# A third weight slab joins the block-by-block start of the two feed-forward layers of an RWKV-7 and pooling decoder step

## The chip, the core and the metric

The kernel runs on one core of a Trainium2 chip, as one program. The metric is the device time in microseconds; lower is better. It is written in Bass: every engine has its own instruction stream, written by hand, and the streams meet only at semaphores that count upwards. TensorE is called PE below, VectorE DVE, ScalarE ACT, GpSimd POOL, and SP is the queue that issues the weight loads.

## What is computed

One inference step of a two-layer trunk for a prompt of 256 tokens and 8 sequences of 4 new tokens, so T = 288 columns. Layer 0 mixes with RWKV-7, layer 1 with causal pooling, and a SwiGLU feed-forward network follows each of them. After every sublayer the residual sum is normalised. Cut to what matters here:

```python
D_MODEL, D_FF = 2048, 5632

def _layer_norm(x, g, b):
    mu = jnp.mean(x, axis=-1, keepdims=True)
    var = jnp.mean(jnp.square(x - mu), axis=-1, keepdims=True)
    return (x - mu) * lax.rsqrt(var + LN_EPS) * g + b

def _swiglu(x, w_in, w_down):
    h = x @ w_in
    gate, up = h[..., :D_FF], h[..., D_FF:]
    return (jax.nn.silu(gate) * up) @ w_down

# in each layer i, after the mixer has given h:
x = _layer_norm(ALPHA * x + h, ln_g[i, 0], ln_b[i, 0])            # norm 0 or norm 2
x = _layer_norm(ALPHA * x + _swiglu(x, ffn_w_in[i], ffn_w_down[i]), ...)
```

## The kernel before

**Layout.** Activations stand with the model dimension on the partitions: X is 16 blocks of 128 x 288. Every matrix product is made from two halves of each operand: the high half is the value rounded to the fp32r type, the low half is the rest. So one 128x128 block of weights times one 128x288 block of activations is three matmuls, written by the helper `three` (lines 727, 728, 729): high x high, high x low, low x high.

**Slabs.** `ffn_w_in` is read in slabs of 2048 x 128 (1 MB): a slab holds the weights of one block of 128 hidden columns, gate and up parts by turns. SP loads slab s into RAW[s % 4] as soon as the low half of slab s - 4 has been taken. ACT writes the high half into WH[:, s % 2] (`hi`, line 1253), and DVE the low half into WL[:, s % 2] (`lo`, line 1683). Since WH and WL have two places, `hi` of slab s waits until PE has used slab s - 2: `act.wait_ge(slab_used, s + 1)`. PE increments `slab_used` with the last matmul of a slab. PE waits for the low half of slab s in `take_slab`. A slab is 16 blocks times 3 matmuls, 48 matmuls.

**The start of a feed-forward layer.** The first three slabs are called s0, s0 + 1 and s0 + 2. Slabs s0 and s0 + 1 stand in the two places of WH and WL. Slab s0 + 2 has places of its own, W3H and W3L, which exist at this one point of each layer. ACT writes W3H in the middle of the norm (`third_hi`, line 1520). DVE writes W3L in `third_lo` (line 2237), after everything that it does for the norm. Slab s0 + 3 goes into WH[:, 1] and WL[:, 1], the place of slab s0 + 1.

**The norms 0 and 2** (`layer_norm`) stand between the mixer and the feed-forward layer. DVE subtracts the mean, ACT squares, PE sums the squares over the partitions (line 1100), ACT takes the root (line 1534), DVE the reciprocal (line 2088). While the root is made, DVE converts what `beside` names: two slabs at norm 0, one slab at norm 2. Then the norm is applied block by block, 16 times: DVE scales (line 2093), ACT adds the bias and writes the high half MH (lines 1538 and 1540), DVE writes the low half ML (line 2098) and increments `ln_lo`. PE follows behind: for each block k it waits for `ln_lo` and then makes the three matmuls of block k for slab s0 and the three for slab s0 + 1. After all 16 blocks it makes slab s0 + 2 in one piece (`third_slab`), and then slab s0 + 3 (`hidden(0, 3)`), which is the first that went through the ordinary rotation of two places.

**Behind it.** ACT takes the sigmoid of each gate block (line 1558), DVE multiplies twice (lines 2180, 2183), ACT and DVE write the halves HH and HL of the hidden block (lines 1560, 2188). ACT's order at the start is: `hi` of s0 + 3, sigmoid, HH, `hi` of s0 + 4, `hi` of s0 + 5.

Of the kernel before, what the change touches and what calls it, by code (L numbers as in the profile page):

```python
# [25 lines left out]
T = SEQ + NS  # L26
# [106 lines left out]
def build(nc, x_prompt, x_sample, state_wkv, state_shift, state_pool, ln_g, ln_b, rw_mu, rw_wr, rw_wk, rw_wv,  # L133
# [4 lines left out]
    with ctx:  # L138
# [585 lines left out]
        def _(pe):  # L724
            def three(out, wh, wl, xh, xl, first, last):

                pe.matmul(out, wh, xh, start=first, stop=False)  # L727
                pe.matmul(out, wh, xl, start=False, stop=False)  # L728
                return pe.matmul(out, wl, xh, start=False, stop=last)  # L729

            def take_slab(s):
                pe.wait_ge(lo_ready, s + 5)

            def take_bank(o):
                pe.wait_ge(out_free, o + 1)
# [388 lines left out]
            def ffn(layer, lnk):  # L1124
                for g in range(2):
                    s0 = SLAB[f"ffn{layer}"] + g * FFN_SLABS
                    o0 = OUT[f"ffn{layer}"] + g * FFN_OUTS

                    def up(j, k):
                        return three(PS[j][:, 0:T], WH[:, j % 2, k * P:(k + 1) * P], WL[:, j % 2, k * P:(k + 1) * P],  # L1130
                                     MH[0][:, k, :], ML[0][:, k, :], k == 0, k == KC - 1)

                    def hidden(i, j):
                        take_slab(s0 + 4 * i + j)
                        take_bank(o0 + 4 * i + j)
                        for k in range(KC):
                            ins = up(j, k)
                        ins.then_inc(slab_used, 1)

                    def third_slab():  # L1140
                        take_slab(s0 + 2)
                        take_bank(o0 + 2)
                        for k in range(KC):
                            ins = three(PS[2][:, 0:T], W3H[:, k * P:(k + 1) * P], W3L[:, k * P:(k + 1) * P],
                                        MH[0][:, k, :], ML[0][:, k, :], k == 0, k == KC - 1)
                        ins.then_inc(slab_used, 1)

                    if g == 0:

                        take_slab(s0 + 1)  # L1150
                        take_bank(o0 + 1)
                        for k in range(KC):
                            pe.wait_ge(ln["lo"], HALVED[lnk] + k + 1)
                            first = up(0, k)
                            second = up(1, k)
                        first.then_inc(slab_used, 1)
                        second.then_inc(slab_used, 1)
                        third_slab()
                        hidden(0, 3)
                    with pe.Fori(1 - g, HG // 2) as i:  # L1160
                        for j in range(4):
                            hidden(i, j)
                    s1, o1 = s0 + 2 * HG, o0 + 2 * HG
                    hidden_before = 2 + (2 * layer + g) * HG
                    pe.wait_ge(hl_ready, hidden_before + HH2)

                    def outputs(i, js):
                        for j in js:
                            c = 4 * i + j // 2
                            take_slab(s1 + 8 * i + j)  # L1170
                            if j % 2 == 0:
                                take_bank(o1 + c)
                            for k in range(HH2):
                                kk = (j % 2) * HH2 + k
                                if kk == HG - 1 and isinstance(i, int):
                                    pe.wait_ge(hl_ready, hidden_before + HG)
                                ins = three(PS[j // 2][:, 0:T], WH[:, j % 2, k * P:(k + 1) * P],
                                            WL[:, j % 2, k * P:(k + 1) * P], HH[:, kk, :], HL[:, kk, :],
                                            kk == 0, kk == HG - 1)
                            ins.then_inc(slab_used, 1)  # L1180
                            if g == 1 and isinstance(i, int) and i > 0 and j == 0:
                                pe.wait_ge(st["x"], 15 * layer + 12)
                                pe.matmul(PS[4][:, 0:T], AVG, SUM[:, :], start=True, stop=True).then_inc(st["c"], 1)

                    outputs(0, range(8))
                    with pe.Fori(1, KC // 4 - g) as i:
                        outputs(i, range(8))
                    if g == 1:
                        outputs(KC // 4 - 1, range(8))
# [489 lines left out]
        def _(dve):  # L1679
# [397 lines left out]
            def layer_norm(k, beside):  # L2077
                n = k // 2
                dve.wait_ge(ln["mean"], n + 1)
                for q in range(4):  # L2080
                    xs = X[:, 4 * q:4 * q + 4, 1:T + 1]
                    dve.tensor_tensor(xs, xs, PS[4][:, 0:T].unsqueeze(1).broadcast_to([P, 4, T]), ALU.subtract)\
                       .then_inc(ln["cen"], 1)
                dve.wait_ge(ln["sq"], 4 * n + 4)
                dve.tensor_tensor(SQ[:, 8:12, :], SQ[:, 8:12, :], SQ[:, 12:16, :], ALU.add).then_inc(ln["pairs"], 1)
                beside()
                dve.wait_ge(ln["sd"], 2 * n + 2)
                dve.reciprocal(LNS[:, 1, :], LNS[:, 0, :]).then_inc(ln["rstd"], 1)
                dve.wait_ge(ln["rstd"], n + 1)
                dve.wait_ge(ln["cen"], 4 * n + 4)  # L2090

                def scaled(c):
                    dve.scalar_tensor_tensor(out=xcur(c), in0=xcur(c), scalar=par("ln_g", k * KC + c),
                                             in1=LNS[:, 1, :], op0=ALU.mult, op1=ALU.mult).then_inc(ln["scaled"], 1)

                def low(c):
                    dve.wait_ge(ln["done"], n * KC + c + 1)
                    dve.tensor_tensor(one(ML[0], c), xcur(c), one(MH[0], c).bitcast(F32), ALU.subtract)\  # L2098
                       .then_inc(ln["lo"], 1)

                for c in range(3):
                    scaled(c)
                with dve.Fori(0, KC - 3) as c:
                    scaled(c + 3)
                    low(c)
                for c in range(KC - 3, KC):
                    low(c)
                third_lo(SLAB["ffn0"] if k == 0 else SLAB["ffn1"])

            def four(q):  # L2110
                return X[:, 4 * q:4 * q + 4, 1:T + 1]
# [123 lines left out]
            def third_lo(s0):  # L2235
                dve.wait_ge(hi_ready, s0 + 3)
                dve.tensor_tensor(W3L[:, :], RAW[:, 2, :], W3H[:, :].bitcast(F32), ALU.subtract).then_inc(lo_ready, 1)
# [127 lines left out]
```

## Time and profile before

| what | value |
|---|---|
| median of 3 runs | 2696.5 us (2691.27 to 2697.71) |
| the profiled execution's own time | 2698.18 us |
| its span in the profile | 2696.6 us |
| PE busy | 2580.0 us, 96% of the span |
| DVE busy | 1577.9 us, 59% |
| ACT busy | 1131.9 us, 42% |
| mean granted PE clock | 0.981 of full |
| chain that ended last | PE 82%, DVE 11%, ACT 3% |

How to read it: PE is the engine that sets the time. A microsecond counts when PE stands still or runs at a lower clock; time on DVE or ACT counts only where PE waits for it. The profile's own time is 1.7 us above the median, within the scatter of the runs. All times below are microseconds from the span's start. Norm 0 lies at about 885 to 917, norm 2 at about 1814 to 1845.

### The profile page before, as it was taken

How to read it: one execution, taken by the hardware profiler on the slowest of the kernel's cores; microseconds unless marked ns; L12 is line 12 of the kernel's file. 1: busy time of each engine (PE TensorE's matmuls, PEld its weight loads, DVE VectorE, ACT ScalarE, POOL GpSimd, SP SyncE). 2: the span in 40 equal slices, each digit the busy share in tenths (PEclk: the TensorE clock that was granted, in tenths of full speed). 3: DMA queues.
4: the chain of work that ended last, by engine and by line, in shares of the span. 5: the costliest groups of instructions: out<-in, count | busy, mean ns of one | idle time of the engine just before them, and what ended most of it. 6: DMA issues, size and time to landing. Idle time of an engine off the chain costs nothing.

```text
span 2696.6 us, 56357 instructions
## 1 busy us (share of the span) xinstructions
PE 2580.0 (96%) x23305; PEld 2480.2 (92%) x23305; DVE 1577.9 (59%) x2400; ACT 1131.9 (42%) x1596; POOL 142.5 (5%) x211
## 2 busy tenths in 40 slices
PE   7989999999999899999999999969999999999997
PEld 7977888888789899999999999958999999999997
DVE  7877888888856644444444444686444444444446
ACT  5565555555533533333333333445333333333334
POOL 0000111111001000000000000100000000000000
PEclk9989999999999999999999999979999999999999
DMA  7622223222336656555665556524555566565563
GB/s 211 184 78 71 77 83 84 84 84 82 91 91 196 156 164 169 161 146 162 188 171 161 166 141 168 175 69 125 165 161 166 144 167 190 160 170 163 142 167 94
DMA packets 707051, 379.33 MB, mean 141 GB/s; under 512 B 16023, under 2 KB 699191, under 8 KB 706711
## 3 DMA queue, kind: packets, MB, share of 16 engines
q1 hardware_dynamic: 701040, 363.46, 48.1%
q0 software_dynamic: 5792, 13.34, 1.8%
q8 instruction: 114, 1.87, 0.3%
q10 hardware_dynamic: 70, 0.39, 0.1%
q14 instruction: 35, 0.29, 0.0%
HBM read 367.31 MB, written 10.62 MB: 140 GB/s over the span
## 4 chain that ended last, share of the span: by engine, by line
PE 82%; DVE 11%; ACT 3%; issue 2%; DMA 1%; SPq 0%; DVEq 0%; POOL 0%; ACTq 0%
PE PS L727 25%; PE PS L728 24%; PE PS L729 24%; PE PS L880 2%; DVE WL L1683 2%; ACT WH L1253 1%; DVE PL L1800 1%; DVE ML L1698 1%; PE PS L912 1%; DVE TM L1691 1%; DMA PR<-in_rw_wk 1%; PE PS L999 0%; PE PS L954 0%; PE PS L917 0%; DVE XL L1939 0%
## 5 line engine op out<-in xcount | busy, mean ns | idle before, releaser
L1683 DVE TENSOR_TENSOR WL<-RAW,WH 128x2048 fp32r<-128x2048 f32 (+1 forms) x325 | 658.6, 2027 | 761.0 <-ACT WH L1253 761.0
L727 PE MATMUL PS<-MH,WH 128*128 128x288 f32 (+1 forms) x3152 | 931.2, 295 | 17.8 <-DVE ML L2098 11.8
L728 PE MATMUL PS<-ML,WH 128*128 128x288 f32 (+1 forms) x3152 | 933.7, 296 | 0.0
L729 PE MATMUL PS<-MH,WL 128*128 128x288 f32 (+1 forms) x3152 | 932.9, 296 | 0.0
L1253 ACT ACTIVATE WH<-RAW 128x2048 fp32r<-128x2048 f32 (+1 forms) x325 | 553.4, 1703 | 824.7 <-PE PS L729 808.5
L727 PEld LDWEIGHTS PS<-MH,WH 128*128 128x128 f32 (+1 forms) x3152 | 595.8, 189 | 22.3 <-issue 13.8
L728 PEld LDWEIGHTS PS<-ML,WH 128*128 128x128 f32 (+1 forms) x3152 | 595.8, 189 | 0.2
L729 PEld LDWEIGHTS PS<-MH,WL 128*128 128x128 f32 (+1 forms) x3152 | 595.0, 189 | 0.0
L728 PE MATMUL PS<-HL,WH 128*128 128x288 f32 x1408 | 415.3, 295 | 0.0
L729 PE MATMUL PS<-HH,WL 128*128 128x288 f32 x1408 | 415.0, 295 | 0.0
L727 PE MATMUL PS<-HH,WH 128*128 128x288 f32 x1408 | 413.4, 294 | 0.0
L727 PEld LDWEIGHTS PS<-HH,WH 128*128 128x128 f32 x1408 | 264.7, 188 | 0.1
L728 PEld LDWEIGHTS PS<-HL,WH 128*128 128x128 f32 x1408 | 264.7, 188 | 0.1
L729 PEld LDWEIGHTS PS<-HH,WL 128*128 128x128 f32 x1408 | 264.5, 188 | 0.0
L727 PE MATMUL PS<-MH,PH 128*128 128x288 f32 x768 | 245.5, 320 | 8.4 <-DVE ML L2028 3.8
L728 PE MATMUL PS<-ML,PH 128*128 128x288 f32 x768 | 230.0, 300 | 0.0
L729 PE MATMUL PS<-MH,PL 128*128 128x288 f32 x768 | 229.1, 298 | 0.0
L727 PEld LDWEIGHTS PS<-MH,PH 128*128 128x128 f32 x768 | 147.2, 192 | 33.5 <-issue 22.2
L728 PEld LDWEIGHTS PS<-ML,PH 128*128 128x128 f32 x768 | 147.7, 192 | 0.3
L1560 ACT ACTIVATE HH<-TM 128x288 f32 (+1 forms) x88 | 39.2, 445 | 258.6 <-DVE TM L2183 258.6
L729 PEld LDWEIGHTS PS<-MH,PL 128*128 128x128 f32 x768 | 147.5, 192 | 0.0
L1800 DVE TENSOR_TENSOR PL<-PR,PH 128x512 fp32r<-128x512 f32 x144 | 92.5, 653 | 51.3 <-ACT PH L1354 50.3
(313 smaller groups left out, 2726.7 us busy)
## 6 DMA issues: line engine op xcount, KB each, us to landing
RAW<-in_ffn_w_in SPq DMA_DIRECT2D x176, 1024.0 KB, 5.7
RAW<-in_ffn_w_down SPq DMA_DIRECT2D x128, 704.0 KB, 4.8
RAW<-in_rw_wr SPq DMA_DIRECT2D x16, 1024.0 KB, 6.5
PR<-in_rw_wk SPq DMA_DIRECT2D x64, 256.0 KB, 3.1
PR<-in_rw_wv SPq DMA_DIRECT2D x64, 256.0 KB, 3.0
PR<-in_rw_wo SPq DMA_DIRECT2D x64, 256.0 KB, 3.2
S0N<-in_state_wkv POOLq DMA_DIRECT2D x64, 64.0 KB, 2.2
out<-SOS POOLq DMA_DIRECT2D x64, 64.0 KB, 2.7
```

The costliest lines, as they stand in the source:

```text
L727: pe.matmul(out, wh, xh, start=first, stop=False)
L728: pe.matmul(out, wh, xl, start=False, stop=False)
L729: return pe.matmul(out, wl, xh, start=False, stop=last)
L880: ins = pe.matmul(bank[hr[r], col + u * CH:col + (u + 1) * CH], lhs(hr[r], u), rhs(hr[r], u), start=True, stop=True)
L912: pe.transpose((PA, PB)[t][:, n * P:(n + 1) * P], f[:, t * P:(t + 1) * P], IDN)
L1253: act.activation(WH[0:rows, j % 2, 0:n], RAW[0:rows, j, 0:n], ACT.Copy).then_inc(hi_ready, 1)
L1560: act.activation(HH[:, bass.ds(hc, 1), :].rearrange("p a t -> p (a t)"), TM[:, b, :], ACT.Copy).then_inc(hh_ready, 1)
L1683: dve.tensor_tensor(WL[0:rows, j % 2, 0:n], RAW[0:rows, j, 0:n], WH[0:rows, j % 2, 0:n].bitcast(F32), ALU.subtract).then_inc(lo_ready, 1)
L1691: dve.scalar_tensor_tensor(out=TM[:, c % 2, :], in0=XX[:, c, :], scalar=PAR[:, row:row + 1], in1=X[:, c, 1:T + 1], op0=ALU.mult, op1=ALU.a ...
L1698: dve.tensor_tensor(ML[m][:, c, :], mixed, MH[m][:, c, :].bitcast(F32), ALU.subtract)\
L1800: dve.tensor_tensor(PL[slot][0:rows, 0:n], PR[slot][0:rows, 0:n], PH[slot][0:rows, 0:n].bitcast(F32), ALU.subtract).then_inc(pc_lo, 1)
```

## The change

Two edits, both at the start of the two feed-forward layers. On PE, slab s0 + 2 no longer follows in one piece: each block now makes nine matmuls, three for each of the slabs s0, s0 + 1, s0 + 2. The matmuls that increment `slab_used` for the three slabs are therefore the last ones of block 15 for each slab. The waits for W3L (`take_slab(s0 + 2)`) and for the third PSUM bank stand ahead of the first block. On DVE, `third_lo` moves from the end of `layer_norm` to the place between `beside()` and the reciprocal. ACT's and SP's streams are the same as before.

```diff
                     if g == 0:
 
-                        take_slab(s0 + 1)
-                        take_bank(o0 + 1)
+                        take_slab(s0 + 2)
+                        take_bank(o0 + 2)
                         for k in range(KC):
                             pe.wait_ge(ln["lo"], HALVED[lnk] + k + 1)
-                            first = up(0, k)
-                            second = up(1, k)
-                        first.then_inc(slab_used, 1)
-                        second.then_inc(slab_used, 1)
-                        third_slab()
+                            ends = [up(0, k), up(1, k), third(k)]
+                        for ins in ends:
+                            ins.then_inc(slab_used, 1)
                         hidden(0, 3)
...
                 beside()
+                third_lo(SLAB["ffn0"] if k == 0 else SLAB["ffn1"])
                 dve.wait_ge(ln["sd"], 2 * n + 2)
                 dve.reciprocal(LNS[:, 1, :], LNS[:, 0, :]).then_inc(ln["rstd"], 1)
...
                 for c in range(KC - 3, KC):
                     low(c)
-                third_lo(SLAB["ffn0"] if k == 0 else SLAB["ffn1"])
```

DVE's stream at norm 0, before the change (LNS is the norm's scale, ML the low half of the normalised block):

```order
L1683 TENSOR_TENSOR WL<-RAW,WH 128x2048 x2
L2088 RECIPROCAL LNS<-LNS 128x288
L2093 SCALAR_TENSOR_TENSOR X<-X,PAR,LNS 128x288 x3
...
L2098 TENSOR_TENSOR ML_61<-X,MH_60 128x288 x3
L2237 TENSOR_TENSOR W3L<-RAW,W3H 128x2048
L1683 TENSOR_TENSOR WL<-RAW,WH 128x2048
L2180 TENSOR_TENSOR TM<-TM,PS 128x288
```

DVE's stream at the same place, after the change (its line numbers are five lower):

```order
L1678 TENSOR_TENSOR WL<-RAW,WH 128x2048 x2
L2232 TENSOR_TENSOR W3L<-RAW,W3H 128x2048
L2084 RECIPROCAL LNS<-LNS 128x288
L2089 SCALAR_TENSOR_TENSOR X<-X,PAR,LNS 128x288 x3
...
L2094 TENSOR_TENSOR ML_61<-X,MH_60 128x288 x3
L1678 TENSOR_TENSOR WL<-RAW,WH 128x2048
L2175 TENSOR_TENSOR TM<-TM,PS 128x288
```

The low half W3L moved from behind the last ML to the place ahead of the reciprocal. Norm 2 has the same two streams with one WL in place of two at the top.

PE's stream at the end of the 16 blocks of norm 0, before (PS0 to PS3 are the banks of the slabs s0 to s0 + 3):

```order
L727 MATMUL PS1<-MH0_60,WH_50 128x288
L728 MATMUL PS1<-ML0_61,WH_50 128x288
L729 MATMUL PS1<-MH0_60,WL_51 128x288
L727 MATMUL PS2<-MH0_60,W3H_175 128x288
L728 MATMUL PS2<-ML0_61,W3H_175 128x288
...
L729 MATMUL PS2<-MH0_60,W3L_176 128x288
L727 MATMUL PS3<-MH0_60,WH_50 128x288
L728 MATMUL PS3<-ML0_61,WH_50 128x288
```

The same place after the change:

```order
L728 MATMUL PS1<-ML0_61,WH_50 128x288
L729 MATMUL PS1<-MH0_60,WL_51 128x288
L727 MATMUL PS2<-MH0_60,W3H_175 128x288
L728 MATMUL PS2<-ML0_61,W3H_175 128x288
L729 MATMUL PS2<-MH0_60,W3L_176 128x288
L727 MATMUL PS3<-MH0_60,WH_50 128x288
L728 MATMUL PS3<-ML0_61,WH_50 128x288
```

Between the last matmul of slab s0 + 1 (PS1) and the first of slab s0 + 3 (PS3) there stood 48 matmuls of slab s0 + 2; now there stand 3.

## Rows read from the trace of the kernel before

**Rows 1.** Costliest groups: busy, mean ns of one | idle before, releaser

```profile
L1683 DVE TENSOR_TENSOR WL<-RAW,WH 128x2048 fp32r<-128x2048 f32 (+1 forms) x325 | 658.6, 2027 | 761.0 <-ACT WH L1253 761.0
L1253 ACT ACTIVATE WH<-RAW 128x2048 fp32r<-128x2048 f32 (+1 forms) x325 | 553.4, 1703 | 824.7 <-PE PS L729 808.5
```

**Rows 2.** PE's waits over the whole span: us in total, times, longest

```profile
PE PS L727 <- DVE ML L2098: 11.8, 2, 6.2
```

**Rows 3.** Timeline, head of norm 0: start, us, engine, line [idle before <-releaser]

```profile
893.51 4.49 DVE L1683 TENSOR_TENSOR WL<-RAW,WH 128x2048 fp32r<-128x2048 f32 x2
...
896.81 0.44 ACT L1534 ACTIVATE LNS<-LNS 128x288 f32<-128x288 f32 x1
897.92 1.95 DVE L2088 RECIPROCAL LNS<-LNS 128x288 f32<-128x288 f32 x1
...
902.53 0.58 PE L727 MATMUL PS<-MH,WH 128*128 128x288 f32 x1 [6.20 <-DVE ML L2098]
```

**Rows 4.** Timeline, head of norm 2

```profile
1822.12 2.28 DVE L1683 TENSOR_TENSOR WL<-RAW,WH 128x2048 fp32r<-128x2048 f32 x1
...
1825.90 1.95 DVE L2088 RECIPROCAL LNS<-LNS 128x288 f32<-128x288 f32 x1 [1.49 <-ACT LNS L1534]
...
1830.50 0.58 PE L727 MATMUL PS<-MH,WH 128*128 128x288 f32 x1 [5.56 <-DVE ML L2098]
```

**Rows 5.** Timeline, the blocks of norm 0 and their end

```profile
909.02 0.45 DVE L2098 TENSOR_TENSOR ML<-X,MH  x1
...
909.89 0.45 DVE L2098 TENSOR_TENSOR ML<-X,MH  x1
...
914.86 2.28 DVE L2237 TENSOR_TENSOR W3L<-RAW,W3H 128x2048 fp32r<-128x2048 f32 x1
...
916.97 0.29 PE L729 MATMUL PS<-MH,WL 128*128 128x288 f32 x1
...
917.20 0.40 PE L727 MATMUL PS<-MH,W3H 128*128 128x288 f32 x1
...
917.37 1.92 ACT L1253 ACTIVATE WH<-RAW 128x2048 fp32r<-128x2048 f32 x1 [2.91 <-PE PS L729]
```

**Rows 6.** Timeline, where slab s0 + 2 begins at norm 2

```profile
1845.28 0.30 PE L727 MATMUL PS<-MH,W3H 128*128 128x288 f32 x1
```

**Rows 7.** Windows: stretch, length, busy of PE, PEld, DVE, ACT, POOL, PEclk, DMA

```profile
907.00:917.00 10.00, 10.00 (x78) 10.00 (x76) 9.28 (x18) 7.45 (x18) 0.00 (x0) 1.00 0.01 2
```

**Rows 8.** Timelines of ACT and of DVE behind slab s0 + 3's high half

```profile
919.30 1.28 ACT L1558 ACT_TABLE_LOAD   x1
...
922.50 0.45 ACT L1560 ACTIVATE HH<-TM 128x288 fp32r<-128x288 f32 x1 [1.49 <-DVE TM L2183]
...
919.32 2.29 DVE L1683 TENSOR_TENSOR WL<-RAW,WH 128x2048 fp32r<-128x2048 f32 x1 [2.17 <-ACT WH L1253]
921.53 0.45 DVE L2180 TENSOR_TENSOR TM<-TM,PS 128x288 f32<-128x288 f32 x1
```

**Rows 9.** Timeline of PE: its first matmul after pauses near 4 us

```profile
175.42 0.61 PE L727 MATMUL PS<-LHH,PH 96*128 96x288 f32 x1 [3.88 <-ACT TM L1386]
...
193.24 0.45 PE L912 MATMUL PS<-CP,AR 128*128 128x128 f32 x1 [4.76 <-DVE BK L1890]
...
853.58 0.58 PE L727 MATMUL PS<-MH,PH 128*128 128x288 f32 x1 [3.77 <-DVE ML L2028]
```

**Rows 10.** Windows: low-clock stretches after five restarts of PE (columns as in rows 7)

```profile
175.42:179.51 4.09, 4.09 (x16) 3.92 (x17) 1.39 (x2) 1.88 (x4) 1.72 (x3) 0.50 0.88 251
...
193.24:199.99 6.75, 6.75 (x44) 6.02 (x48) 1.48 (x3) 2.17 (x6) 0.00 (x0) 0.50 0.30 87
...
853.58:858.76 5.18, 5.18 (x22) 5.18 (x23) 1.92 (x3) 0.63 (x1) 0.82 (x1) 0.50 0.00 0
...
902.53:906.55 4.02, 4.02 (x17) 4.02 (x18) 4.02 (x10) 4.02 (x10) 0.00 (x0) 0.50 0.51 131
...
1830.50:1834.97 4.47, 4.47 (x19) 4.47 (x20) 4.47 (x11) 4.47 (x11) 0.00 (x0) 0.50 0.01 4
```

More of the change, by code:

```diff
@@ L1138, in hidden, with third @@
                         ins.then_inc(slab_used, 1)
-                    def third_slab():
+                    def third(k):
+                        return three(PS[2][:, 0:T], W3H[:, k * P:(k + 1) * P], W3L[:, k * P:(k + 1) * P],
+                                     MH[0][:, k, :], ML[0][:, k, :], k == 0, k == KC - 1)
+                    if g == 0:
                         take_slab(s0 + 2)
@@ L1143, in third_slab @@
                         for k in range(KC):
[L1144 to L1148, printed above, removed]
-                        take_slab(s0 + 1)
-                        take_bank(o0 + 1)
-                        for k in range(KC):
-                            pe.wait_ge(ln["lo"], HALVED[lnk] + k + 1)
-                            first = up(0, k)
-                            second = up(1, k)
-                        first.then_inc(slab_used, 1)
-                        second.then_inc(slab_used, 1)
-                        third_slab()
+                            pe.wait_ge(ln["lo"], HALVED[lnk] + k + 1)
+                            ends = [up(0, k), up(1, k), third(k)]
+                        for ins in ends:
+                            ins.then_inc(slab_used, 1)
                         hidden(0, 3)
```

## The prediction, as it went on record before the changed kernel ran

> **What bounds the kernel now.** I read the page's shares first: PE is busy for nearly the whole span, so the only questions are where PE waits, what its clock is, and what the edits do to either. Second the list of PE's waits. For the matmuls of line 727 behind the norms' low halves it shows 11.8 us in two waits [rows 2]. The timelines of the two norms name these two: 6.20 us ahead of the first block at 902.53 [rows 3] and 5.56 us at 1830.50 [rows 4], together 11.76. So nothing is left for blocks 1 to 15: once begun, PE never waits for the norm. The reader is to see why. A low half leaves DVE every 0.87 us (909.02, then 909.89) [rows 5]. PE takes 78 matmuls in 10.00 us at full clock, with the first and last cut by the window, so about 0.132 us each [rows 7], and 6 x 0.132 = 0.79 us a block. That is a little quicker than DVE, but PE begins at half clock for 4.02 and 4.47 us [rows 10], falls behind there, and never catches up. At the end of the blocks PE's last matmul of slab s0 + 1 starts at 916.97 and the first of slab s0 + 2 at 917.20, 0.23 apart where 0.13 is the pace [rows 5]: the wait for W3L cost 0.10 us at norm 0. At norm 2 the matmuls of slab s0 + 2 begin at 1845.28 with no wait named [rows 6]. All that the new order can remove is therefore 0.1 us.
>
> **The change, part by part.**
>
> Matmuls: the same number, the same operands. An output now gets its block in turns of three, where it got them in turns of two or in one piece; before, the interleaved part ran at 0.132 us a matmul [rows 7], so the order itself costs nothing. Nine matmuls take 1.19 us a block against 0.87 us of the norm: PE stays behind the norm, no wait, no gain.
>
> W3L ahead of the reciprocal. DVE converts two slabs at norm 0 from 893.51, and the reciprocal starts at 897.92 without an idle remark, (897.92 - 893.51) / 2 = 2.20 us for each conversion. The root was ready at 896.81 + 0.44 = 897.25 [rows 3], so DVE has no slack there and a third conversion moves the reciprocal, the first block and PE's restart by 2.20 us. At norm 2 DVE idles 1.49 us ahead of the reciprocal [rows 4]. The conversions would start at 1822.12 and 1824.32, the reciprocal at 1826.52 and not at 1825.90: 0.62 us. What took 2.28 us behind the last ML [rows 5] is gone there, but it was hidden under PE's matmuls: worth the 0.10 us and no more. RAW[2] comes free some 17 us earlier; SP loads slab s0 + 6 earlier. The loads are hidden anyway (ACT's 824.7 us of idling ahead of the high halves are 808.5 us waits for PE [rows 1]).
>
> The two places of WH and WL. This is the largest step. Slab s0 + 3 wants slab s0 + 1's place. Before, ACT could begin at 917.37, 0.40 us after the start of that slab's last matmul [rows 5], and had the 48 matmuls of slab s0 + 2, 48 x 0.132 = 6.3 us, as cover for 1.92 us on ACT and 2.29 us on DVE (from 919.32) [rows 5, 8]. Now slab s0 + 1 ends 3 matmuls ahead of slab s0 + 2 and the cover is gone. Count from the start of the last matmul of slab s0 + 2. The last one of slab s0 + 1 starts 3 x 0.132 = 0.40 earlier, so ACT starts at 0.00. DVE starts 919.32 - 917.37 = 1.95 later and takes 2.29: 4.24. PE starts 0.06 after a low half is done (917.20 against 914.86 + 2.28 = 917.14) [rows 5]: 4.30. The next matmul would have come at 0.13, so 4.17 us are lost, a pause of 4.30 - 0.29 = 4.0 us, at each of the two norms. Queued behind the late work: on ACT the sigmoid's table load and the high half of slab s0 + 4, on DVE the two products. Before, HH ends 922.50 + 0.45 - 917.37 = 5.58 after ACT's start [rows 8]. Slab s0 + 4 then needs 1.92 + 0.03 + 2.29, ready at 9.82. PE needs it at 4.30 + 6.3 = 10.6 at full clock. So the second slab is just in time, by 0.8 us, and later ones fall back into the old rhythm.
>
> The clock. Three pauses of this size stand in the trace: 3.88, 4.76 and 3.77 us [rows 9]. After each the granted clock is 0.50, the 1.2 GHz level, for 4.09, 6.75 and 5.18 us of matmuls; after the norms' own pauses, 6.20 and 5.56 us long, for 4.02 and 4.47 [rows 10]. No pause of nearly 4 us passed without it. At half clock half of the time is lost: the mean over the five is 24.51 / 5 = 4.90 us, 2.45 us lost; the ends are 4.02 / 2 = 2.0 and 6.75 / 2 = 3.4. I take 2.45 for each new pause, 0 as the bound below.
>
> The Trainium skill, in TensorE: Matmul & The Clock Gate, section HAM oscillation, says that a loop should do all its K tiles for one output before it waits, or each wait throws the array back to half rate. By that rule the new order, three outputs side by side and then a wait for all, is the wrong way round; its worked example has 1.67 us at half rate for each restart, an estimate of 0.83 us lost, which would make the sum 12.8. This trace's restarts are longer, so the sum goes by them.
>
> The norms' own restart: the half-clock stretch at the first block exists already (4.02 and 4.47). A start 2.20 us later can meet it differently. If the clock rose at the same moment as before, 1.10 + 0.31 us would be given back; if the stretch grew to the longest seen, 6.75, it would cost 1.37 + 1.14 more. I take nothing, and keep both ends.
>
> **Sum.** Norm 0: 2.20 - 0.10 + 4.17 + 2.45 = 8.72. Norm 2: 0.62 + 4.17 + 2.45 = 7.24. Together 16.0 us on the profiled execution's 2698.18 us. The median of the runs shown is 1.7 us lower, so the forecast for a median is 2696.5 + 16.0 = 2712.5 us, 0.6% slower. A difference of 0.3%, about 8.1 us, is what a measurement of this kernel tells from none.
>
> **The rivals.**
>
> A. The pauses come, the clock doesn't fall in them: 16.0 - 4.9 = 11.1, 2707.6 us. For it: the pause of 4.0 us is among the shortest of the group. Against it: all three neighbours fell. 10 in 100.
>
> B. Not slower by what can be told. The mechanism: earlier W3L frees RAW[2], and if the weight loads were what ended the waits in the feed-forward layers, one slab time of 6.3 us less at each layer would come off: 16.0 - 12.6 = 3.4, 2699.9 us, within 0.3%. It decides from the point where more than 4 us a layer are DMA waits. Against it: at most 824.7 - 808.5 = 16.2 us of ACT's waits in the whole kernel are for anything but PE [rows 1]. 5 in 100.
>
> C. Faster: PE is starved in blocks 1 to 15 after all, and the third slab fills the holes. A PE at full clock from 902.53 would end 96 matmuls at 915.2 and not at 917.2, so 2.0 us a norm is all that there is to fill; it decides only if holes exceed 8 us a norm. To flip the sign it also needs the pause not to occur, so 2 in 100: 2696.5 - 4.1 = 2692.4 us.
>
> D. Worse: slab s0 + 4 comes late too, or the half-clock stretches are all of the longest kind: 1.9 us for the two new ones, 2.5 at the norms' starts, 1 us or so a norm for slab s0 + 4: 16.0 + 6.4, 2719 us. The cover of 0.8 us is thin, but half clock on slab s0 + 3 widens it to 3. 7 in 100.
>
> The forecast itself: 76 in 100; its own range is 16.0 - 1.4 - 0.9 to 16.0 + 2.5 + 1.9, 2710.2 to 2716.9.
>
> **How the numbers follow.** The overall range takes in A's 2707.6 with its give-back of 1.4 below, and above reaches 2717, half a microsecond or so being runs against runs: 2706 to 2717.5. Left out are B and C (7 in 100), most of D, and the edges of the rest, some 18 in 100. Slower by over 0.3% means above 2704.6: forecast, A (nearly all) and D, 0.92. Within 0.3%: B and a rest of A, 0.06. Faster: 0.02.
>
> **What would show it.** In the changed profile: the reciprocal of norm 0 starts right behind three conversions, 2.2 us later relative to the root; at norm 2 the idle remark ahead of it is gone. The first matmul of slab s0 + 3 carries an idle remark of about 4.0 us, released by DVE's WL, at both norms; two new low-clock stretches follow, so the list of PE's waits grows by some 8 us in a row "L727 <- DVE WL". No wait stands at the blocks 1 to 15 or at slab s0 + 4. The prediction is wrong if ACT's high half of slab s0 + 3 starts before the last block ends, if the clock stays up through the pause, or if a later wait (the weight loads, the pooling layer) shrinks by what was lost here.

## The result and the profile after

The changed kernel takes 2711.2 us (median of 4 runs, 2710.78 to 2712.75), the kernel before 2696.13 us beside it. The ratio is 1.006, with an interval of 1.0043 to 1.0077: slower by 15.1 us. The forecast was 2712.5 us, 16.0 over before. The profiled execution of the changed kernel took 2712.75 us, with a span of 2711.2. One execution of the last version below, 9797.21 us long, is left out of its ratio but counted in its median of 11; without it that median is 2695.18.

The timelines of DVE at the head of norm 0 and of norm 2, after the change (start, us, engine, line; line numbers are five lower than before):

```profile
892.85 4.49 DVE L1678 TENSOR_TENSOR WL<-RAW,WH 128x2048 fp32r<-128x2048 f32 x2
897.25 2.28 DVE L2232 TENSOR_TENSOR W3L<-RAW,W3H 128x2048 fp32r<-128x2048 f32 x1
899.46 1.95 DVE L2084 RECIPROCAL LNS<-LNS 128x288 f32<-128x288 f32 x1
...
1829.58 2.29 DVE L1678 TENSOR_TENSOR WL<-RAW,WH 128x2048 fp32r<-128x2048 f32 x1
1831.78 2.29 DVE L2232 TENSOR_TENSOR W3L<-RAW,W3H 128x2048 fp32r<-128x2048 f32 x1
1833.98 1.95 DVE L2084 RECIPROCAL LNS<-LNS 128x288 f32<-128x288 f32 x1
```

They answer to [rows 3, 4]: three conversions stand in a row at norm 0, two at norm 2, and the idle remark ahead of norm 2's reciprocal is gone.

PE's first matmuls of the blocks and of slab s0 + 3, at norm 0 and at norm 2, from PE's timeline:

```profile
904.07 0.58 PE L727 MATMUL PS<-MH,WH 128*128 128x288 f32 x1 [7.90 <-DVE ML L2094]
...
925.50 0.29 PE L729 MATMUL PS<-MH,W3L 128*128 128x288 f32 x1
929.78 0.54 PE L727 MATMUL PS<-MH,WH 128*128 128x288 f32 x1 [3.99 <-DVE WL L1678]
...
1838.59 0.58 PE L727 MATMUL PS<-MH,WH 128*128 128x288 f32 x1 [6.42 <-DVE ML L2094]
...
1860.31 0.29 PE L729 MATMUL PS<-MH,W3L 128*128 128x288 f32 x1
1864.67 0.40 PE L727 MATMUL PS<-MH,WH 128*128 128x288 f32 x1 [4.08 <-DVE WL L1678]
```

Two new pauses of 4 us, released by DVE's low half of slab s0 + 3. Nothing of the kind stood there before: slab s0 + 3 simply followed slab s0 + 2. From 925.50 to 929.78 is 4.28, where 0.13 is the pace: 4.15 lost. At norm 2 it is 1864.67 - 1860.31 - 0.13 = 4.23. ACT's timeline shows the start of the chain behind the first of them:

```profile
925.50 1.91 ACT L1248 ACTIVATE WH<-RAW 128x2048 fp32r<-128x2048 f32 x1 [9.51 <-PE PS L729]
927.42 1.28 ACT L1553 ACT_TABLE_LOAD   x1
928.72 0.41 ACT L1553 ACTIVATE TM<-PS 128x288 f32<-128x288 f32 x1
930.62 0.44 ACT L1555 ACTIVATE HH<-TM 128x288 fp32r<-128x288 f32 x1 [1.49 <-DVE TM L2178]
930.96 1.89 ACT L1248 ACTIVATE WH<-RAW 128x2048 fp32r<-128x2048 f32 x1
```

ACT had idled 9.51 us and begins at 925.50, in the instant in which PE starts its last matmul of slab s0 + 2. The clock, by windows (length, busy of the engines, then the granted clock, then DMA):

```profile
904.07:909.41 5.34, 5.34 (x22) 5.34 (x23) 5.34 (x13) 5.34 (x13) 0.00 (x0) 0.50 0.71 174
929.89:933.30 3.41, 3.41 (x15) 3.41 (x16) 1.52 (x4) 2.24 (x2) 0.00 (x0) 0.50 0.98 201
1838.59:1844.66 6.07, 6.07 (x25) 6.07 (x26) 6.07 (x15) 6.07 (x15) 0.00 (x0) 0.50 0.36 87
1865.14:1868.56 3.42, 3.42 (x17) 3.42 (x16) 1.57 (x3) 2.24 (x2) 0.00 (x0) 0.50 0.79 216
```

The stretches at the head of the blocks are longer than in [rows 10] (5.34 and 6.07 against 4.02 and 4.47), and each new pause has one of 3.4 us behind it.

**Where the time went.** To compare kernels I cut each norm in three by PE's timeline. A: from the first matmul of the sums of squares (line 1100) to the first of block 0. B: from there to the first matmul of slab s0 + 3; it holds the 144 matmuls of three slabs. C: the 96 matmuls from there, two slabs. The last column but one is how long the granted clock stayed at 0.50 behind the first block. All in us, norm 0 / norm 2, from the one profiled execution of each kernel; "over before" is A + B + C less that of the kernel before, first norm 0, then norm 2:

| kernel | A | B | C | half clock from the first block on | over before |
|---|---|---|---|---|---|
| before | 13.97 / 13.34 | 21.17 / 21.17 | 12.70 / 12.70 | 4.02 / 4.47 | |
| changed | 16.17 / 13.96 | 25.71 / 26.09 | 14.34 / 14.33 | 5.34 / 6.07 | 8.38 and 7.17, 15.55 in all |
| W3L early alone | 16.17 / 13.96 | 21.69 / 21.56 | 12.70 / 12.70 | 5.61 / 5.20 | 2.71 and 1.00 |
| twelve blocks behind | 16.18 / 13.96 | 21.54 / 21.28 | 12.70 / 12.70 | 5.23 / 4.67 | 2.58 and 0.73 |
| six blocks behind | 16.17 / 13.95 | 23.37 / 22.37 | 12.80 / 12.80 | 5.46 / 3.08 | 4.50 and 1.91 |
| pause alone | 13.97 / 13.34 | 25.66 / 25.72 | 15.35 / 15.38 | 4.06 / 4.16 | 7.14 and 7.23 |
| pause filled, 11 | 16.17 / 13.97 | 26.87 / 25.67 | 12.91 / 12.91 | 5.85 / 3.17 | 8.11 and 5.33 |
| pause filled, 7 | 16.17 / 13.95 | 25.67 / 25.11 | 12.80 / 12.81 | 5.25 / 3.89 | 6.80 and 4.65 |
| warm norms | 13.97 / 12.85 | 21.18 / 21.18 | 12.70 / 12.70 | 3.41, late / none | 0.00 and -0.48 |
| W3L on POOL | 18.40 / 14.10 | 20.50 / 19.65 | 12.70 / 12.70 | 2.99 / none | 3.76 and -0.76 |
| last version | 13.97 / 13.97 | 21.17 / 19.51 | 12.70 / 12.70 | none / none | 0.00 and -1.03 |

The stretch between the two norms (880.5 to 880.8 us) and the one behind C of norm 2 (832.2 us before and after the change) are the same to 0.3 us in all of them. The stretch ahead of norm 0 is not: its sums of squares begin at 888.56 before, at 887.89 after the change, and anywhere from 883.60 to 889.13 in the other runs. That scatter of 5.5 us is why kernels are compared by this table and by medians, and not by the length of one execution.

### The profile page after: what moved, and what is told of

Read it like the earlier page. It is cut to its first block, busy times and chain, and to the rows that moved or that the text cites. A ratio compares the mean times of both kernels' runs of the same rounds, so it can differ in the third digit from the quotient of the medians.

```text
span 2711.2 us, 56355 instructions
## 1 busy us (share of the span) xinstructions
PE 2585.0 (95%) x23305; PEld 2484.6 (92%) x23305; DVE 1578.2 (58%) x2400; ACT 1131.3 (42%) x1596; POOL 142.2 (5%) x211
## 3 DMA queue, kind: packets, MB, share of 16 engines
q0 software_dynamic: 5792, 13.34, 1.8%
## 4 chain that ended last, share of the span: by engine, by line
PE 81%; DVE 12%; ACT 3%; issue 2%; DMA 1%; SPq 0%; DVEq 0%; POOL 0%; ACTq 0%
PE PS L727 24%; PE PS L728 24%; PE PS L729 24%; PE PS L880 2%; DVE WL L1678 2%; ACT WH L1248 1%; DVE PL L1795 1%; DVE ML L1693 1%; DVE TM L1686 1%; PE PS L912 1%; PE PS L999 1%; PE PS L954 0%; PE PS L949 0%; DVE XL L1934 0%; PE PS L917 0%
## 5 line engine op out<-in xcount | busy, mean ns | idle before, releaser
L727 PE MATMUL PS<-MH,WH 128*128 128x288 f32 (+1 forms) x3152 | 932.2, 296 | 30.1 <-DVE ML L2094 14.3
L729 PE MATMUL PS<-MH,WL 128*128 128x288 f32 (+1 forms) x3152 | 933.5, 296 | 0.0
L727 PEld LDWEIGHTS PS<-MH,WH 128*128 128x128 f32 (+1 forms) x3152 | 596.6, 189 | 35.5 <-issue 16.4
L729 PEld LDWEIGHTS PS<-MH,WL 128*128 128x128 f32 (+1 forms) x3152 | 595.7, 189 | 0.0
L729 PE MATMUL PS<-HH,WL 128*128 128x288 f32 x1408 | 415.2, 295 | 0.0
L727 PE MATMUL PS<-HH,WH 128*128 128x288 f32 x1408 | 413.6, 294 | 0.0
L727 PEld LDWEIGHTS PS<-HH,WH 128*128 128x128 f32 x1408 | 265.0, 188 | 0.1
L729 PEld LDWEIGHTS PS<-HH,WL 128*128 128x128 f32 x1408 | 264.6, 188 | 0.0
L727 PE MATMUL PS<-MH,PH 128*128 128x288 f32 x768 | 245.9, 320 | 8.4 <-DVE ML L2023 3.8
L729 PE MATMUL PS<-MH,PL 128*128 128x288 f32 x768 | 229.3, 299 | 0.0
L727 PEld LDWEIGHTS PS<-MH,PH 128*128 128x128 f32 x768 | 147.5, 192 | 33.4 <-issue 22.4
L729 PEld LDWEIGHTS PS<-MH,PL 128*128 128x128 f32 x768 | 147.7, 192 | 0.0
```

## The experiments

The theory: three terms add up, a later first block (the DVE edit), a pause ahead of slab s0 + 3 (the place of slab s0 + 1 comes free 45 matmuls later), and half clock behind the pause. The rivals: one edit alone carries the loss, the interleaved order is slow in itself, or the clock has another cause.

**W3L early alone**

```diff
                 beside()
+                third_lo(SLAB["ffn0"] if k == 0 else SLAB["ffn1"])
...
                 for c in range(KC - 3, KC):
                     low(c)
-                third_lo(SLAB["ffn0"] if k == 0 else SLAB["ffn1"])
```

> The kernel before with only the DVE edit: W3L ahead of the reciprocal at both norms, PE's order as before (slab s0 + 2 in one piece behind the 16 blocks). Theory (three terms add up: the late reciprocal, the pause ahead of slab s0 + 3, the half clock behind it): only the first term is left, 2.20 us at norm 0 and 0.62 at norm 2, less the 0.10 us wait for W3L; 2.7 us over before (0.1%), give or take 1 us of half clock at the norms' restart. PE has no pause ahead of slab s0 + 3. Rival 1 (the DVE edit carries most of the loss, by what it delays behind the reciprocal): 8 us or more over before. Rival 2 (the 2.2 us are taken up by later waits): no difference anywhere in the alignment of the two traces behind norm 0.

2699.74 us, ratio 1.0015 (1.0005 to 1.0024), 3.4 us over before. By the table A grows by 2.20 and 0.62, as worked out, and B by 0.52 and 0.39. The first term is right, and it is not taken up later (between the norms lie 880.5 us, before 880.8): rivals 1 and 2 fall. B was expected to shrink by 0.1. Its window shows why it grew: PE spends 5.61 us at half clock at the head of norm 0, 1.59 more than before.

```profile
904.04:909.65 5.61, 5.61 (x23) 5.61 (x24) 5.61 (x13) 5.61 (x14) 0.00 (x0) 0.50 0.68 165
```

**Twelve blocks behind.** The changed kernel, where slab s0 + 2 trails:

```diff
-                            ends = [up(0, k), up(1, k), third(k)]
+                            ends = [up(0, k), up(1, k)]
+                            if k >= 12:
+                                last = third(k - 12)
                         for ins in ends:
                             ins.then_inc(slab_used, 1)
+                        for k in range(KC - 12, KC):
+                            last = third(k)
+                        last.then_inc(slab_used, 1)
```

> The changed kernel, with slab s0 + 2 twelve blocks behind the other two: block k makes the matmuls of block k for s0 and s0 + 1 and of block k - 12 for s0 + 2; 36 matmuls of s0 + 2 are left behind block 15, and slab_used of s0 and s0 + 1 is incremented ahead of them. They are 36 x 0.132 = 4.75 us of cover, where 4.24 + 0.06 - 0.40 are wanted. Theory: no pause ahead of slab s0 + 3, no half clock there, the same time as with the DVE edit alone (2.7 us over before), though the third slab is interleaved in four blocks. Rival 1 (turns of three banks, or W3H among WH, slow the matmuls themselves): still several us over that.

2699.59 us, ratio 1.0012 (1.0003 to 1.0021). The pause is gone; PE's timeline at the passage from slab s0 + 2 to slab s0 + 3 of norm 0, and ACT's start of the high half:

```profile
923.93 0.29 PE L729 MATMUL PS<-MH,W3L 128*128 128x288 f32 x1
924.07 0.29 PE L727 MATMUL PS<-MH,WH 128*128 128x288 f32 x1
...
919.13 1.92 ACT L1253 ACTIVATE WH<-RAW 128x2048 fp32r<-128x2048 f32 x1 [4.69 <-PE PS L729]
```

ACT starts 4.9 us ahead of slab s0 + 3 and the passage runs at the pace of 0.13. What is left is the DVE edit alone to within 0.4 us (3.31 against 3.71 by the table). So 36 of the 48 matmuls behind the release are cover enough.

**Six blocks behind.** The same edit with 6 in place of 12.

> The changed kernel with slab s0 + 2 six blocks behind the other two, so 18 matmuls, 18 x 0.132 = 2.4 us, stand between the release of slab s0 + 1's place and slab s0 + 3. Theory: the pause shrinks by just that, 4.17 - 2.4 = 1.8 us a norm; with the DVE edit's 2.7 that is 2.7 + 3.6 = 6.3 us over before if the clock stays up, and up to 2 x 1.7 more if so short a pause (1.6 us of idle) still brings the clock down. Rival (turns of three cost by themselves, since more blocks are interleaved than with twelve behind): more than 9.7.

2702.04 us, ratio 1.002 (1.0011 to 1.0029), 5.0 us over before; 6.41 by the table, against 6.3 expected. PE's timeline at slab s0 + 3, norm 0 and norm 2, and the windows behind it:

```profile
927.32 0.40 PE L727 MATMUL PS<-MH,WH 128*128 128x288 f32 x1 [1.60 <-DVE WL L1683]
...
1857.12 0.40 PE L727 MATMUL PS<-MH,WH 128*128 128x288 f32 x1 [1.68 <-DVE WL L1683]
...
927.32:931.00 3.68, 3.68 (x28) 3.68 (x29) 1.78 (x4) 2.25 (x2) 0.00 (x0) 1.00 0.97 224
1857.12:1861.00 3.88, 3.88 (x29) 3.88 (x30) 1.99 (x4) 2.25 (x2) 0.00 (x0) 1.00 0.63 187
```

The idle time fell from 4.0 to 1.6 us, by the 2.4 us of 18 matmuls, and behind so short a pause the clock stayed at 1.00 both times. That the total comes so near 6.3 is in part luck: the half clock at the head was 5.46 us long at norm 0 and only 3.08 at norm 2. With the run before it this is the pause as a function of the cover: none at 36 matmuls, 1.6 at 18, 4.0 at none. Interleaving ten blocks cost nothing of its own, which the third expected sentence asked.

**Pause alone.** The kernel before, and one wait more on ACT:

```diff
                             if not (g == 0 and isinstance(i, int) and i == 0 and j == 0):
+                                if g == 0 and isinstance(i, int) and i == 0 and j == 1:
+                                    act.wait_ge(slab_used, s0 + 5)
                                 hi(s0 // 4 + i + (j + 2) // 4, (j + 2) % 4, s0 + 4 * i + j + 2,
```

> The kernel before, with one wait of ACT made later and nothing else: the high half of slab s0 + 3 waits until slab s0 + 2 is used as well. W3L stands where it stood, PE's order is that of before. Theory: the pause alone gives most of the loss. ACT starts 0.40 us after the start of the last matmul of s0 + 2, so PE starts 4.70 after it where 0.13 is the pace, 4.57 lost, and 1.65 of half clock, at each of two norms: 12.4 us over before. Rival 1 (the interleaved order or the early W3L is the cause): under 9 us. Rival 2 (slab s0 + 4 comes late too): over 14 us, with a second idle remark one slab later.

2710.57 us, ratio 1.0055 (1.0041 to 1.0068), 14.3 us over before. Neither edit of the change is in this kernel, and a loss nearly as large is. It isn't the same sum: here the pause and the half clock behind it are the whole 14.37 us of the table, with pauses 0.3 us longer (4.33 and 4.40 against 3.99 and 4.08), since ACT waits for a matmul three places later; in the changed kernel they are 8.38 + 3.27 = 11.65 of 15.55, the rest coming with early W3L. B grows by 4.49 and 4.55 (expected 4.57), C by 2.65 and 2.68 (expected 1.65): the half clock behind the pause lasted longer than in the changed kernel.

```profile
926.14 0.61 PE L727 MATMUL PS<-MH,WH 128*128 128x288 f32 x1 [4.33 <-DVE WL L1685]
...
926.14:931.85 5.71, 5.71 (x24) 5.71 (x25) 3.51 (x4) 2.24 (x2) 0.00 (x0) 0.50 1.07 232
1861.35:1867.10 5.75, 5.75 (x24) 5.75 (x25) 3.51 (x4) 2.24 (x2) 0.00 (x0) 0.50 0.65 182
```

At half clock the matmuls start 0.24 us apart, where 12.70 / 96 = 0.132 is the pace, so not half but 45% of such a stretch is lost: 0.45 x 5.71 = 2.57, and 0.10 for the first matmul, against C's growth of 2.65. The total lies above the 14 us that I had set as the mark of rival 2, but no idle remark stands one slab later, and the clock accounts for it; rival 2 falls.

**Pause filled, with 11 and with 7 matmuls.** The changed kernel and, ahead of slab s0 + 3:

```diff
+                        for _ in range(7):
+                            pe.matmul(PS[7][:, 0:T], AVG, CP[:, 0:T], start=True, stop=True)
                         hidden(0, 3)
```

The first of the two runs had 11 and read block 0 of X. Bank 7 is read by nobody, so the outputs don't depend on them.

> The changed kernel with 11 added matmuls between block 15 and slab s0 + 3 (a 128x128 constant in 32 bits times block 0 of X, into PSUM bank 7, which nobody reads). Each takes 0.33 us at full clock in the norm's sums, together 3.6 us of the pause of 4.0. Theory: the pause in the work stays, 4.17 us, but the clock doesn't fall, so the 3.4 us low-clock stretch behind each pause (929.89 to 933.30 and 1865.14 to 1868.56 in the changed kernel's trace) is gone: 2 x 1.65 = 3.3 us quicker than the changed kernel, some 11.5 over before. Rival (the low stretch has another cause, such as the power of the dense blocks ahead): the stretches stay, and the time is the changed kernel's, 15 us over before.

> As the run with 11 added matmuls, with 7 (a 128x128 constant in 32 bits times 288 constant columns, into bank 7, which nobody reads). That run showed 0.25 us for each half of such a matmul, 0.5 for a matmul: 11 of them took 5.25 us in a pause of 4.0 and held slab s0 + 3 up, while the low-clock stretches were gone. 7 take 3.5 us and leave room. Theory: the pause in the useful work stays 4.17 us, the low stretches of 3.4 us behind it are gone, so 2 x 1.65 = 3.3 us quicker than the changed kernel: 11.8 over before. Rival (the clock would cost nothing here, or the added matmuls cost as much as they give): 15 over before, as the changed kernel.

With 11: 2711.55 us, ratio 1.0052 (1.0038 to 1.0065), no gain that can be told. The added matmuls held the place from 927.06 to 932.18, 5.12 us, where 4.28 are free. I had misread the row by which I sized them: a matmul in 32 bits stands in the trace as two records, 0.25 us each at full clock. The clock stayed at 1.00 behind them at both norms: ```profile
927.06 5.50 PE L1155 MATMUL PS<-X,CP 128*128 128x288 f32 x22
932.18 0.51 PE L727 MATMUL PS<-MH,WH 128*128 128x288 f32 x1
...
932.18:936.00 3.82, 3.82 (x30) 3.77 (x29) 2.13 (x2) 2.11 (x2) 0.00 (x0) 1.00 1.04 227
```

With 7: 2707.42 us, ratio 1.0034 (1.0022 to 1.0046), 10.3 over before. PE's timeline and the window behind it:

```profile
924.20 3.56 PE L1155 MATMUL PS<-CP 128*128 128x288 f32 x14
928.36 0.40 PE L727 MATMUL PS<-MH,WH 128*128 128x288 f32 x1 [0.60 <-DVE WL L1680]
...
928.36:932.00 3.64, 3.64 (x27) 3.64 (x28) 1.74 (x4) 2.25 (x2) 0.00 (x0) 1.00 0.98 215
```

At norm 0 slab s0 + 3 comes no sooner, but runs at full clock: C is 12.80 where it was 14.34. By the table this kernel is 4.10 us quicker than the changed one, by the medians 3.8 (4.7 where each is set against the kernel before beside it). C is 3.1 of it (1.54 + 1.52). Nearly all the rest is B of norm 2, 0.98, and there the half clock at the head was 3.89 us long and not 6.07: 0.45 x 2.18 = 0.98. The added matmuls stand behind it and can't have done that. So the half clock behind the pause comes from PE's idleness and costs 1.5 us a norm.

**Warm norms.** The kernel before, 4 matmuls on constants ahead of the sums of squares and 10 behind them.

```diff
+                for _ in range(4):
+                    pe.matmul(PS[7][:, 0:T], AVG, CP[:, 0:T], start=True, stop=True)
                 for q in range(3):
...
                 ins.then_inc(ln["var"], 1)
+                for _ in range(10):
+                    pe.matmul(PS[7][:, 0:T], AVG, CP[:, 0:T], start=True, stop=True)
```

> The kernel before, with matmuls on constants in PE's two idle stretches of each norm: 4 ahead of the sums of the squares, 10 behind them (bank 7, read by nobody). They should keep the granted clock at 1.00 in the first blocks, where it was 0.50 for 4.02 and 4.47 us. Theory (before, slab s0 + 2 had to wait for W3L, done at 917.14, and slab s0 at half clock merely used up that time): the first blocks run at full clock, a wait of about 2 us for W3L appears, and the time is that of before within 1 us. Rival (the half clock at the norms' start is on the path): 2.0 + 2.2 = 4.2 us quicker.

2695.53 us, ratio 0.9993 (0.9984 to 1.0002), no difference that can be told. The window at the head of norm 2 has full clock; at norm 0 the clock fell all the same, a little later, with a mean of 0.63:

```profile
902.58:906.58 4.00, 4.00 (x19) 3.89 (x20) 4.00 (x10) 4.00 (x10) 0.00 (x0) 0.63 0.54 135
1830.09:1834.09 4.00, 4.00 (x27) 3.77 (x28) 4.00 (x10) 4.00 (x10) 0.00 (x0) 1.00 0.00 0
```

B is 21.18 at both, as before. At norm 2 PE was warm from the first block and gained nothing by it, since slab s0 + 2 waited for W3L:

```profile
1844.76 0.40 PE L727 MATMUL PS<-MH,W3H 128*128 128x288 f32 x1 [0.80 <-DVE W3L L2241]
```

I had expected a wait of 2 us there; it is 0.80, the rest goes into short gaps between the blocks. The last version below shows the same at norm 0: full clock at the head, a wait of 0.76 for W3L, B 21.17. So taking away the half clock at the head would have given the kernel before nothing: B was set by DVE's 16 blocks and W3L behind them. With W3L early this bound is gone, and B follows the length of the half clock.

**W3L on POOL,** with warm norms and three blocks of slab s0 + 2 taken in behind blocks 6, 10 and 14:

```diff
+            def third_low(s0):
+                pool.wait_ge(hi_ready, s0 + 3)
+                pool.tensor_tensor(W3L[:, :], RAW[:, 2, :], W3H[:, :].bitcast(F32), ALU.subtract).then_inc(third_ready, 1)
...
                             second = up(1, k)
+                            if k in (6, 10, 14):
+                                if k == 6:
+                                    pe.wait_ge(third_ready, layer + 1)
+                                third_slab([k // 4 - 1])
```

> A version made from the kernel before, meant to beat both: W3L is written by POOL, idle in both norms (it takes 0.8 us for 288 columns, so about 5.5 us for 2048, from 894.0 to 899.5), and DVE has neither the 2.20 us ahead of the reciprocal nor the 2.28 us behind the last ML; PE is kept warm in the norms as in the run with added matmuls; three blocks of slab s0 + 2 are taken in behind blocks 6, 10 and 14 to fill the holes of a warm PE, and 13 blocks (5.1 us) are left to cover slab s0 + 3's conversion. Theory: the half clock's 2.0 and 2.2 us come off, so about 4 us quicker than before (0.15%), with no pause anywhere. Rival 1 (POOL slows DVE's conversions or norm while it works on W3L): little or no gain, and longer rows of DVE in the norm. Rival 2 (added matmuls delay the sums or the first block): slower than before.

2700.31 us, ratio 1.0011 (1.0002 to 1.002), slower than before. Timelines of DVE and of POOL at norm 0:

```profile
892.26 8.92 DVE L1697 TENSOR_TENSOR WL<-RAW,WH 128x2048 fp32r<-128x2048 f32 x2
...
894.46 6.71 DVE L1697 TENSOR_TENSOR WL<-RAW,WH 128x2048 fp32r<-128x2048 f32 x1
...
892.83 6.20 POOL L716 TENSOR_TENSOR W3L<-RAW,W3H 128x2048 fp32r<-128x2048 f32 x1 [9.06 <-ACT W3H L1534]
```

Two conversions of DVE that took 4.49 us took 8.92 while POOL worked for 6.20. A grows by 4.43, which is just that: rival 1, and more of it than I had thought. At norm 2, where less of DVE's work met POOL's, A grows by 0.76 only. B falls to 19.65 there, at full clock and with no wait for W3L.

**The last version.** Norm 0 as before; at norm 2 W3L early on DVE, three blocks of slab s0 + 2 behind blocks 4, 9 and 14; warm norms.

```diff
                 beside()
+                if k == 2:
+                    third_lo(SLAB["ffn1"])
...
                             second = up(1, k)
+                            if layer == 1 and k in (4, 9, 14):
+                                third_slab([k // 5])
```

> What the runs point to, meant to beat both kernels. Norm 0 stays as before (W3L late, slab s0 + 2 in one piece), since DVE has no slack there. At norm 2, where it has 1.49 us, W3L is made ahead of the reciprocal on DVE, PE takes blocks 0, 1, 2 of slab s0 + 2 behind blocks 4, 9 and 14, and 13 blocks are left as cover. At both norms constants are multiplied in PE's idle stretches (4 and 10 matmuls, as in the warm run, which showed full clock at the first block and no gain, since slab s0 + 2 waited for W3L). Theory: norm 0 unchanged; at norm 2 the first block comes 0.1 us later than before (0.6 later for the conversion, 0.5 earlier for the quicker sums), and the blocks and slab s0 + 2 take about 19.6 us where they took 21.17, so 1.4 us off the kernel, 0.05%, to be seen in the trace and not in a median. Rival (a warm PE catches the norm up and waits as long as before): no difference at norm 2.

2695.44 us against 2695.83 for before beside it, ratio 0.9996 (0.9987 to 1.0006): not to be told from before, and 15 us below the changed kernel. At norm 0 A and B are those of before, though the clock was 1.00 from the first block. B of norm 2 is 19.51, 1.66 less; A is 13.97, 0.63 more, so 1.03 us is gained and not 1.4. PE's timeline at slab s0 + 2 of norm 0, at the first block of norm 2 and at slab s0 + 3, and the windows at the head of both norms:

```profile
912.23 0.40 PE L727 MATMUL PS<-MH,W3H 128*128 128x288 f32 x1 [0.76 <-DVE W3L L2247]
...
1826.19 0.37 PE L727 MATMUL PS<-MH,WH 128*128 128x288 f32 x1 [1.81 <-DVE ML L2107]
...
1845.57 0.29 PE L729 MATMUL PS<-MH,W3L 128*128 128x288 f32 x1
1845.70 0.29 PE L727 MATMUL PS<-MH,WH 128*128 128x288 f32 x1
...
897.57:901.57 4.00, 4.00 (x27) 3.75 (x28) 4.00 (x10) 4.00 (x10) 0.00 (x0) 1.00 0.53 140
1826.19:1830.19 4.00, 4.00 (x28) 3.79 (x29) 4.00 (x10) 4.00 (x10) 0.00 (x0) 1.00 0.52 126
```

The quicker sums of the warm run give nothing here: with two conversions in a row DVE, not the root, sets the reciprocal.

## Why the prediction was right

The mechanism, the place of both pauses and their size came as forecast. The total came closer than its terms deserve: two of them were mis-sized in opposite directions, and that is luck.

**What bounds it, and the gain.** Right. PE did not wait in blocks 1 to 15, before or after, so the new order had nothing to fill; rival C never had a place.

**W3L ahead of the reciprocal.** 2.20 and 0.62 us were worked out from the spacing of the conversions and DVE's idle remark; A shows 2.20 and 0.62, in the changed kernel and with the edit alone.

**The place of slab s0 + 1.** 4.17 us forecast, 4.15 and 4.23 read from PE's timeline. PE's waits for DVE's WL grew from 1.7 us in 3 waits to 9.7 us in 5, the 8 us named as a sign. B of the changed kernel over B of the DVE edit alone is 4.02 and 4.53; the two kernels differ in the half clock at the head too (5.34 against 5.61, 6.07 against 5.20), which makes up the differences. The pause without either edit gave 4.49, where 4.57 was worked out; with 18 and 36 matmuls of cover it shrank as the sum says.

**Slab s0 + 4 just in time.** Right. Its high half starts on ACT at 930.96, no idle remark of PE follows in the two slabs at either norm, and C is explained by the clock.

**The clock.** The mechanism was right, the size wrong. This is the first mis-sized term. I took 2.45 us for each new pause, the mean of half the five stretches in [rows 10]. The changed kernel paid 1.64 and 1.63, below the 2.0 that I had as the lower end of the sizes seen; the pause alone paid 2.65 and 2.68. Two things made it smaller: the stretches were 3.41 and 3.42 us long, not 4.90, and half clock costs 45% of a stretch and not half (0.24 us a matmul against 0.132): 0.45 x 3.41 + 0.10 = 1.63. The list of pauses near 4 us in [rows 9] also lacked one, 3.95 us ahead of 20.28, with half clock behind it too. In the changed kernel at norm 2 the clock fell only at 1865.14, half a microsecond after PE had restarted at 1864.67.

**The norms' own restart.** Sized at nothing; it cost 0.39 at norm 0 and 0.69 at norm 2 (B, 25.71 - 21.17 - 4.15 and 26.09 - 21.17 - 4.23). This is the second mis-sized term, and the step that failed: the sum lets the half clock at the head keep its length, and it grew from 4.02 and 4.47 us to 5.34 and 6.07. At 45% that is 0.59 and 0.72 more. At norm 0 0.20 of it was made good, since slab s0 + 2 no longer waits for W3L (0.10, which the sum has as a term of its own) and no longer starts slowly behind that wait. The prediction did name both ends, and what was paid lies between them.

Whether the change makes the stretch longer is shown at norm 0 alone: the six kernels with early W3L on DVE have 5.23 to 5.85 us there, the two others without added matmuls 4.02 and 4.06. At norm 2 the six scatter from 3.08 to 6.07, around the 4.47 and 4.16 of the two, so that the 0.69 in the profiled execution may as well be its own. Why the stretches differ stays open.

The two mis-sized terms offset each other for the greater part: 4.90 + 0 forecast, 3.27 + 1.08 measured. By the table the change costs 15.55 us, by the medians 15.1. Rival A (no half clock behind the pauses) falls by the windows. B (weight loads) falls by the stretches between and behind the norms, which lost no slab time. D falls by C: no slab behind came late.

By the Trainium skill, TensorE: Matmul & The Clock Gate, section HAM oscillation, a loop should do all K tiles for one output before it waits. The traces agree in direction: the version with 36 of slab s0 + 2's matmuls left behind the release has no pause at all. But the order of the loop isn't what decides here: the pause alone has slab s0 + 2 in one piece and half clock all the same, and six blocks behind has ten of its blocks interleaved and full clock. For the size, the estimate from the page's example was 0.83 us for each restart, and here 1.6 to 2.7 were paid; the measurement decides.

## What to carry to other kernels

Work that seems only to stand in the way can be the cover of a buffer's turn-over. Before merging it into the loop ahead, ask when the last reader of each buffer ends, and who must refill it: here 4.3 us of conversion were hidden under 6.3 us of matmuls, and merging those cost the whole of it. If PE already runs without a wait behind a producer, giving it more to do per block gains nothing, unless what slowed it (here half clock, and the wait for W3L behind it) is taken away too: only with both gone did B of norm 2 fall, from 21.17 to 19.51. A lag of some blocks keeps both, the interleaving and the cover.

## What the runs showed of the hardware

Pauses of 4.0 to 4.4 us of PE were followed by half clock in all four cases at slab s0 + 3 in the changed kernel and in the pause alone, for 3.4 to 5.75 us of matmuls; two pauses of 1.60 and 1.68 us there were followed by none. In the kernel before, idle times of 2.09 us (ahead of 161.35) and 2.26 us (ahead of 1793.36) were followed by half clock too, from 162.44 and from 1794.01 on, 1.09 and 0.65 us into the work. In the warm run the clock fell behind an idle time of only 1.82 us at norm 0, and behind 1.82 and 1.81 us in the last version it did not, so the length of the last pause does not decide it alone; what does is open.

Matmuls on constants in a pause kept the clock up: 7 of them in 32 bits (14 records) took 3.56 us and left slab s0 + 3 at full clock, worth 1.5 us a norm.

While POOL subtracted 128 x 2048 in 6.20 us, two subtractions of DVE took 8.92 us where they take 4.49. The first, begun 0.57 us ahead of POOL's, took its usual 2.29; the second took 6.71 and ended at 901.17, 2.14 us after POOL's 899.03. So it was held up until POOL was done. At norm 2 the same shows on smaller work:

```profile
1825.22 6.17 POOL L716 TENSOR_TENSOR W3L<-RAW,W3H 128x2048 fp32r<-128x2048 f32 x1 [82.21 <-ACT W3H L1534]
1827.95 1.95 DVE L2102 RECIPROCAL LNS<-LNS 128x288 f32<-128x288 f32 x1 [1.02 <-ACT LNS L1548]
...
1829.94 1.77 DVE L2107 SCALAR_TENSOR_TENSOR X<-X,PAR,LNS 128x288 f32<-128x288 f32 x1
```

The reciprocal, with one input, ran inside POOL's work in its usual 1.95 us. The scaling behind it, with two (X and LNS), took 1.77 us where it takes 0.52, and ended 0.32 us after POOL. The Trainium skill, GPSIMD Engine Reference, section Specifications, says that GpSimd's SBUF interfaces are shared with VectorE and that they contend with its instructions that have two inputs in SBUF. The trace agrees with it, with 4.43 us of delay for 6.20 us of POOL's work.
